# Expert weights in eleven slots at the start, selection of tokens in halves, and a TensorE product in each ranking round

## The chip, the cores and the metric

The kernel runs on one core of a Trainium2 chip. The metric is the device time of one execution in microseconds (us). Three executions of the kernel before took 2456.19, 2457.54 and 2457.84 us, with a median of 2457.54.

## The reference, cut to what matters

Two transformer blocks run one after the other on 512 tokens of width 1024. The change touches only the end of the second block: the router, the experts and the last layer norm.

```python
def expert_choice_ffn(x, w_router, w_gate_up, w_down):
    cap = EC_CAPACITY_FACTOR * T // N_EXPERTS            # 2 * 512 // 16 = 64
    logits = einsum('btd,de->bte', x, w_router)
    aff = softmax(logits, axis=-1)                       # 512 tokens x 16 experts
    gate, idx = lax.top_k(swapaxes(aff, 1, 2), cap)      # each expert takes its 64 best tokens
    xs = x[bidx, idx]
    h = einsum('becd,edf->becf', xs, w_gate_up)          # 1024 -> 2048, per expert
    hg, hu = split(h, 2, axis=-1)
    ye = einsum('becf,efd->becd', silu(hg) * hu, w_down) # 1024 -> 1024
    return zeros_like(x).at[bidx, idx].add(ye * gate)

x = layer_norm(DN_ALPHA * x + mix, ln1_g, ln1_b)
ffn = expert_choice_ffn(x, w_router, w_gate_up, w_down)
x = layer_norm(DN_ALPHA * x + ffn, ln2_g, ln2_b)
```

## The kernel before, in words

Everything is float32 on one core. After the first block and the attention of the second, the stage that matters here begins at about 1907 us of the span. It runs in this order.

**Layer norm and router.** The product with w_out_2 ends in the signal `m31`, the normalised rows stand in `XR` (signal `x31` for the last of them), and the logits are ready with `logits`. VectorE makes the affinities `affN` (L3029 to L3034), and TensorE transposes them into a bank, 16 experts by 512 tokens (L2169, signal `affT`).

**Selection.** VectorE ranks in eight rounds over 16 partitions of 512 elements: `max` gives the eight best (L3038), `match_replace` overwrites them with -1 (L3039). What has become negative is chosen; a running sum (`tensor_tensor_scan`, L3042) numbers the chosen tokens, TensorE turns the numbers back to token order (L2173, signal `posN`), and `choose(0)` builds the selection matrix `SP` (L3056) and the gate matrix `SG` (L3058). While VectorE ranks, TensorE has nothing to do.

**Experts.** Experts are taken in pairs, p = 0 to 7. In each pair TensorE does four groups `q` of gate-and-up products (`rows`, L2251), gathers the next pair's tokens (`gather`, L2198), turns the activations (L2284), does two halves of the down product (`down`, L2289), and scatters the results (L2235, L2236); VectorE adds them to `acc` (L3104). In pair 0 the gather (`first_gather`, L2184) is exact and interleaved with the groups.

**Weights.** A pair needs 12 pieces of 2 MB, so there are 96 pieces, c = 0 to 95. They come through a ring of nine slots (`eslot`, `ES = 9`). SyncE issues all loads in one order, and each waits for the group that used its slot nine pieces ago (L690), so piece 20 waits for `group5.0` and pieces 21 and 22 for `group0.1`. Pieces 0 to 2 are issued after `br23.1` (1907 us), then the two rows of the first layer norm's gain and bias (`ln1_g_2`, `ln1_b_2`, L683, into the upper half of `acc`), pieces 3 to 6 after `m31`, piece 7 after `logits`, piece 8 after `posN`; its slot shares its memory with the ranking's tiles. Pieces 9 and 10 come in halves after `half0.0` and `group0.0`.

**Residual and end.** Right after `choose(0)` VectorE writes the scaled residual, ALPHA times the normalised row with gain and bias, into `acc` (`residual`, L3131 and L3133). In the last pair TensorE reads `acc` into the eight output banks with identity products (`kept`, L2220): two of them stand ahead of the last group `q = 3` of gate-and-up, the others around the down products. The last norm then works from those banks.

Of the kernel before, what the change touches and what calls it, by code (L numbers as in the profile page):

```python
# [5 lines left out]
F32, F32R = mybir.dt.float32, mybir.dt.float32r  # L6
# [6 lines left out]
NT = SEQ // P  # L13
# [85 lines left out]
def build(nc, T, out):  # L99
    with ExitStack() as ctx:  # L100
# [3 lines left out]
        def sig(name, step=1):  # L104
            return Sig(nc, ctx, name, step)
# [20 lines left out]
        def carve(t, start, shapes):  # L126
# [97 lines left out]
        (slot4, SGT, SP, xst, ga, actT, ye, acc, posN, affN, m8, lmax, lsum, slot8), at_e = carve(work, 0, [  # L224
            (KB, 512), (512,), (NT, P), (KB, P), (2, 512), (KB, P), (2, 512), (NT, DM),
            (NT, NE), (NT, NE), (8,), (NT,), (NT,), (KB, 512)])
        (affT, wrk, cum), _ = carve(work, at_e - 4096, [(512,), (512,), (512,)])
        assert at_e <= 17560
        lnrow = acc[:, 2:4, :]
        (slot5, slot6, iota, wr, wr2, wb, ln_col), at_e = carve(work, 17560, [(KB, 512), (KB, 512), (EC,), (KB, NE), (KB, HB), (NE,), (2, KB)])  # L230
        fold, wr_b = cols[:, 0:NE], cols[:, 32:160].rearrange("p (k e) -> p k e", k=KB)
        assert at_e <= 26500
        (SG,), at_e = carve(const, 2 * P, [(NT, P)])
        assert at_e <= 6 * P
        SPT, ye_hi, ye_lo, lgT = SGT, ye, ga, cum
# [3 lines left out]
        eslot = [slot5, slot6, ring[2], ring[0], ring[1], ring[3], slot4, AT, slot8]  # L239
        ES = len(eslot)  # L240
        lnrow2 = eslot[(12 * NE // 2 - 8) % ES].rearrange("p k n -> p (k n)")[:, 0:2 * DM].rearrange("p (a b) -> p a b", a=2)

        LAST = 12 * NE // 2 - 2

        def weights(c, at):

            return eslot[c % ES].rearrange("p k n -> p (k n)")[:, at:at + 512]
# [37 lines left out]
        e_w, e_h = [sig(f"expert_weights{q}", 16) for q in range(ES)], [sig(f"expert_halves{q}", 16) for q in range(2)]  # L285
# [174 lines left out]
        def _(sp):  # L460
# [203 lines left out]

            def load_half(sem, c, h, what):
                to, part = eslot[c % ES].rearrange("p k n -> p (k n)"), slice(h * 2048, h * 2048 + 2048)
                sem.mark(sp.dma_start(to[:, part], expert_rows(c // 12, c % 12)[:, part]), what)
            for c in range(12 * NE // 2):
                if c in (ES, ES + 1):
                    if c == ES:  # L670
                        for h in range(2):
                            sp.wait_ge(*e_pe(("half0.0", "group0.0")[h]))
                            for e in range(2):
                                load_half(e_w[(c + e) % ES], c + e, h, f"h{c + e}" if h == 0 else f"w{c + e}")
                    continue
                if c >= ES:
                    sp.wait_ge(*e_pe(f"group{(c - ES) % 12 // 2}.{(c - ES) // 12}"))
                elif c < 3:
                    sp.wait_ge(*mg_pe("br23.1"))
                elif c < 7:  # L680
                    if c == 3:
                        for n, name in enumerate(("ln1_g_2", "ln1_b_2")):
                            l_row.mark(sp.dma_start(lnrow[:, n, :], T[name].broadcast_to([P, DM])), name)  # L683
                    sp.wait_ge(*l_pe("m31"))
                elif c == 7:
                    sp.wait_ge(*q_pe("logits"))
                else:
                    sp.wait_ge(*q_pe("posN"))
                if c < LAST:
                    e_w[c % ES].mark(sp.dma_start(eslot[c % ES].rearrange("p k n -> p (k n)"), expert_rows(c // 12, c % 12)), f"w{c}")  # L690
                elif c == LAST:
                    sp.wait_ge(*e_pe(f"group{(c + 1 - ES) % 12 // 2}.{(c + 1 - ES) // 12}"))
                    for h in range(2):
                        for e in range(2):
                            load_half((e_h if h == 0 else e_w)[e if h == 0 else (c + e) % ES], c + e, h, f"{'hw'[h]}{c + e}")
# [132 lines left out]
        def _(act):  # L828
# [684 lines left out]
            for q in range(4):  # L1513
                first_T(q)
                high(act, e_act, XH[:, q, :], XR[:, q, :], f"XH{q}")
# [20 lines left out]
        def _(pe):  # L1536
# [631 lines left out]
            for t in range(NT):  # L2168
                mm = pe.transpose(psum[3][0:NE, t * P:(t + 1) * P], affN[:, t, :], ident)  # L2169
            q_pe.mark(mm, "affT")  # L2170
            pe.wait_ge(*q_vec("pos"))
            for t in range(NT):
                mm = pe.transpose(psum[2][:, t * NE:(t + 1) * NE], cum[0:NE, t * P:(t + 1) * P], ident[0:NE, 0:NE])  # L2173
            q_pe.mark(mm, "posN")
# [65 lines left out]
            def experts(p):  # L2240
                last = p == NE // 2 - 1

                def loaded(q):
                    for e in range(2):
                        c = 12 * p + 2 * q + e
                        pe.wait_ge(*e_w[c % ES](f"w{c}"))
# [7 lines left out]
                for q in range(4):  # L2254
# [20 lines left out]
                    if p == 0 and q == 0:  # L2275
                        e_pe.mark(mm, "half0.0")
# [27 lines left out]
                for k in range(4):  # L2304
                    for n in range(2):
                        mm = down(0, k, n)
                e_pe.mark(mm, f"group4.{p}")
# [31 lines left out]
        def _(dve):  # L2339
# [685 lines left out]
            q_vec.link(dve, dve.memset(affT[0:NE, :], 1.0))  # L3025
# [20 lines left out]
            q_vec.link(dve, dve.tensor_copy(posN, psum[2][:, 0:NT * NE].rearrange("p (t e) -> p t e", t=NT)))  # L3046
# [13 lines left out]
            def experts(p):  # L3060
# [7 lines left out]
                if not last:  # L3068
                    choose(p + 1)
                if p == 0:  # L3070
# [20 lines left out]
                for m in range(2 * NT):  # L3091
# [4 lines left out]
                    elif last:  # L3096
                        final_stats(t)
                        if t:
                            final_inv(t - 1)
                    else:  # L3100
                        a = acc[:, t, n * 512:(n + 1) * 512]
                        if p:
                            dve.wait_ge(*e_vec(f"acc{m}.{p - 1}"))
                        e_vec.mark(dve.tensor_tensor(a, psum[scatter_banks[m]][:, :], a, ALU.add), f"acc{m}.{p}")  # L3104
# [24 lines left out]
            def residual(t, tmp):  # L3129
                n = XR[:, t, :].rearrange("p (j q) -> p q j", j=KB)  # L3130
                q_vec.link(dve, dve.scalar_tensor_tensor(tmp.rearrange("p (q j) -> p q j", j=KB), n, ALPHA, lnrow[:, 0, :].rearrange("p (q j) -> p q j", j=KB),  # L3131
                                                         ALU.mult, ALU.mult))
                q_vec.mark(dve.scalar_tensor_tensor(acc[:, t, :], lnrow[:, 1, :], ALPHA, tmp, ALU.mult, ALU.add), f"acc{t}")  # L3133
            choose(0)
            dve.wait_ge(*l_row("ln1_b_2"))
            y_row = ye.rearrange("p a n -> p (a n)")
            residual(0, acc[:, 0, :])
            residual(1, acc[:, 1, :])
            dve.wait_ge(*l_act("x31"))
            q_vec.link(dve, dve.scalar_tensor_tensor(y_row.rearrange("p (q j) -> p q j", j=KB), XR[:, 3, :].rearrange("p (j q) -> p q j", j=KB), ALPHA,  # L3140
                                                     lnrow[:, 0, :].rearrange("p (q j) -> p q j", j=KB), ALU.mult, ALU.mult))
            residual(2, acc[:, 2, :])
            q_vec.mark(dve.scalar_tensor_tensor(acc[:, 3, :], lnrow[:, 1, :], ALPHA, y_row, ALU.mult, ALU.add), "acc3")
            for t in range(NT):
                dve.wait_ge(*q_vec(f"acc{t}"))
# [104 lines left out]
```

## Time and profile before

| | before |
|---|---|
| median of three executions | 2457.54 us |
| the profiled execution's own time | 2456.17 us |
| its span | 2454.4 us |
| TensorE busy (matmul) | 2373.1 us, 97% |
| VectorE busy | 1137.8 us, 46% |
| ScalarE busy | 869.1 us, 35% |
| DMA, mean over the span | 163 GB/s |
| expert weights | 96 pieces of 2 MB |

A matmul's end is modelled in the trace, so a busy TensorE is not TensorE at its peak. The share of busy time is a mean over stages with different limits, and the stage of the change is the last fifth of the span. PEclk is the granted TensorE clock as a share of 2.4 GHz: 1.00 is 2.4 GHz and 0.50 is 1.2 GHz.

### The profile page before, as it was taken

How to read it: one execution, taken by the hardware profiler on the slowest of the kernel's cores; microseconds unless marked ns; L12 is line 12 of the kernel's file. 1: busy time of each engine (PE TensorE's matmuls, PEld its weight loads, DVE VectorE, ACT ScalarE, POOL GpSimd, SP SyncE). 2: the span in 40 equal slices, each digit the busy share in tenths (PEclk: the TensorE clock that was granted, in tenths of full speed). 3: DMA queues.
4: the chain of work that ended last, by engine and by line, in shares of the span. 5: the costliest groups of instructions: out<-in, count | busy, mean ns of one | idle time of the engine just before them, and what ended most of it. 6: DMA issues, size and time to landing. Idle time of an engine off the chain costs nothing.

```text
span 2454.4 us, 31324 instructions
## 1 busy us (share of the span) xinstructions
PE 2373.1 (97%) x13306; PEld 1760.8 (72%) x13306; DVE 1137.8 (46%) x1595; ACT 869.1 (35%) x1403; POOL 124.3 (5%) x130
## 2 busy tenths in 40 slices
PE   8999999999999999999999999998999979999997
PEld 6788878888887888888888888865788733443332
DVE  6857676354543324354344463668433552131113
ACT  7554544243433323243233343347322411111111
POOL 0303021100000000000000001200000000000000
PEclk9999999999999999999999999999999989999998
DMA  5121313232224333242222332321322589999996
GB/s 168 70 73 67 104 54 111 70 121 87 102 86 155 120 108 136 79 158 79 93 103 103 112 138 103 115 105 48 127 96 78 200 346 416 429 427 430 428 429 260
DMA packets 117386, 400.97 MB, mean 163 GB/s; under 512 B 6656, under 2 KB 24704, under 8 KB 104320
## 3 DMA queue, kind: packets, MB, share of 16 engines
q1 hardware_dynamic: 113088, 384.29, 40.7%
q0 software_dynamic: 4160, 14.68, 1.7%
q8 instruction: 106, 1.74, 0.3%
q14 instruction: 32, 0.26, 0.0%
HBM read 385.06 MB, written 13.89 MB: 163 GB/s over the span
## 4 chain that ended last, share of the span: by engine, by line
PE 83%; DVE 7%; DMA 6%; ACT 3%; issue 1%; SPq 0%; POOL 0%; DVEq 0%; ACTq 0%; POOLq 0%
PE banks L94 20%; PE banks L96 19%; PE banks L95 19%; PE banks L2251 7%; PE banks L2289 5%; DMA activations_T<-w_gate_up_in 1%; DMA ring<-w_gate_up_in 1%; DMA work<-w_gate_up_in 1%; DVE ring_split L88 1%; DMA work<-o_b 1%; PE banks L1653 1%; DMA ring<-w_up_in 1%; PE banks L1665 1%; PE banks L2030 1%; PE banks L1683 1%
## 5 line engine op out<-in xcount | busy, mean ns | idle before, releaser
L94 PE MATMUL banks<-work_split,ring_split 128*128 128x512 f32 (+1 forms) x1560 | 617.4, 396 | 2.4 <-issue 0.8
L88 DVE TENSOR_TENSOR ring_split<-ring,halves_split 128x1024 fp32r<-128x1024 f32 x281 | 353.5, 1268 | 523.3 <-ACT halves_split L83 522.9
L95 PE MATMUL banks<-work_split,halves_split 128*128 128x512 f32 x1512 | 588.8, 389 | 0.0
L96 PE MATMUL banks<-activations_T_split,halves_split 128*128 128x512 f32 x1160 | 452.3, 390 | 0.0
L83 ACT ACTIVATE halves_split<-ring 128x1024 fp32r<-128x1024 f32 x281 | 293.7, 1055 | 310.9 <-PE banks L96 236.5
L94 PEld LDWEIGHTS banks<-work_split,ring_split 128*128 128x128 f32 x1560 | 293.0, 188 | 70.1 <-issue 8.1
L95 PEld LDWEIGHTS banks<-work_split,halves_split 128*128 128x128 f32 x1512 | 284.1, 188 | 55.7 <-issue 0.5
L96 PE MATMUL banks<-ring_split,work_split 128*128 128x512 f32 (+1 forms) x704 | 270.8, 385 | 0.0
L95 PE MATMUL banks<-halves_split,work_split 128*128 128x512 f32 x672 | 261.6, 389 | 0.0
L96 PEld LDWEIGHTS banks<-activations_T_split,halves_split 128*128 128x128 f32 x1160 | 217.7, 188 | 46.2
L2251 PE MATMUL banks<-work 128*64 128x512 f32 x464 | 150.7, 607 | 4.9 <-DMA work<-w_gate_up_in 2.6
L94 PE MATMUL banks<-halves_split,work_split 128*128 128x512 f32 x384 | 150.1, 391 | 1.9 <-DVE ring_split L88 1.9
L96 PEld LDWEIGHTS banks<-ring_split,work_split 128*128 128x128 f32 x704 | 132.2, 188 | 26.4
L95 PEld LDWEIGHTS banks<-halves_split,work_split 128*128 128x128 f32 x672 | 126.2, 188 | 25.7
L96 PE MATMUL banks<-work_split,halves_split 128*128 128x512 f32 x352 | 137.0, 389 | 0.0
L88 DVE TENSOR_TENSOR work_split<-work,work_split 128x1024 fp32r<-128x1024 f32 (+2 forms) x98 | 101.6, 1066 | 36.7 <-ACT work_split L83 36.7
L94 PE MATMUL banks<-halves_split,activations_T_split 128*128 128x512 f32 x288 | 114.7, 398 | 0.0
L3078 DVE TENSOR_TENSOR work<-banks,work 128x512 f32<-128x512 f32 x16 | 10.3, 687 | 198.1 <-ACT work L1498 198.1
L2251 PE MATMUL banks<-ring,work 128*64 128x512 f32 x336 | 94.6, 609 | 5.1 <-DMA ring<-w_gate_up_in 2.8
L2251 PEld LDWEIGHTS banks<-work 128*64 128x64 f32 x464 | 47.2, 140 | 72.7 <-issue 72.7
L83 ACT ACTIVATE work_split<-work 128x1024 fp32r<-128x1024 f32 (+2 forms) x98 | 87.9, 926 | 29.3 <-PE banks L1702 10.5
L1498 ACT ACTIVATE work<-banks 128x512 f32<-128x512 f32 x16 | 8.7, 597 | 251.9 <-PE banks L2251 251.9
(387 smaller groups left out, 3166.6 us busy)
## 6 DMA issues: line engine op xcount, KB each, us to landing
ring<-w_in_in SPq DMA_DIRECT2D x30, 2048.0 KB, 7.7
work<-w_gate_up_in SPq DMA_DIRECT2D x29, 2048.0 KB, 26.8
ring<-w_gate_up_in SPq DMA_DIRECT2D x21, 2048.0 KB, 26.2
ring<-w_down_in SPq DMA_DIRECT2D x19, 2048.0 KB, 9.2
work<-w_down_in SPq DMA_DIRECT2D x11, 2048.0 KB, 27.0
ring<-w_in_in SPq DMA_DIRECT2D x17, 1024.0 KB, 7.7
ring<-w_up_in SPq DMA_DIRECT2D x8, 2048.0 KB, 7.9
activations_T<-w_gate_up_in SPq DMA_DIRECT2D x8, 2048.0 KB, 26.9
```

The lines of the kernel that those rows point to most:

```text
L83: s.mark(act.activation(R(dst), src, ACT.Copy), what)
L88: s.mark(dve.tensor_tensor(R(dst), src, R(hi).bitcast(F32), ALU.subtract), what)
L94: pe.matmul(out, R(ll), R(rh), start=start, stop=False)
L95: pe.matmul(out, R(lh), R(rh), start=False, stop=False)
L96: return pe.matmul(out, R(lh), R(rl), start=False, stop=stop)
L1653: mm = pe.matmul(bank_a[j][x, c], NMd[j][h, t, :], Yd[j][h, t, :], start=True, stop=True)
L1665: x_mm = pe.matmul(bank_b[j][x, c], PP[j][x, t, :], X[j][x, t, :], start=True, stop=True)
L1683: mm = pe.matmul(V, Y[j][:, t, :], vb[:, j, t, :], start=True, stop=(t == 0))
L2030: mm = pe.transpose(turned_at(fam, i)[:, s, k * P:(k + 1) * P], probs_at(fam, i)[:, s, k * P:(k + 1) * P], ident)
L2251: mm = pe.matmul(psum[3 + c % 2 * 2 + c // 2][64 * e:64 * e + 64, :], xst[:, 2 * q + k, 64 * e:64 * e + 64], weights(12 * p + 2 * q + e, k ...
L2289: mm = pe.matmul(psum[4 + n][64 * e:64 * e + 64, :], actT[:, 4 * a + k, 64 * e:64 * e + 64], weights(12 * p + 8 + 2 * a + e, k * DM + n * ...
L3078: e_vec.mark(dve.tensor_tensor(g, psum[4 + 2 * f][:, :].rearrange("p (q k) -> p k q", k=4), g, ALU.mult), f"ga{f}.{p}")
```

## The change

1. **Slots.** Two more regions serve as weight slots, each once: `XH` (the high parts of the rows, not needed before pair 0's gathers) holds piece 0, `acc` holds piece 10. After that the ring has nine slots as before, in the order given by `slot_no` and `former`. Four pieces are issued after `br23.1`, pieces 4 to 7 and 10 after `m31`, piece 8 after `logits`, piece 9 after `x31`. During pair 0 the next loads are issued in halves.
2. **Residual.** Since `acc` holds weights in pair 0, the residual is no longer written first. Pair 0's results are copied into `acc` (no add). The gain and bias rows are loaded into `XH` late, between the issues of pieces 90 and 91, behind a wait for `whole3`: four additions on VectorE in pair 6 that restore the full rows in `XR`. The residual is then added in `keep()`, on VectorE in the last pair, and `kept(n, t)` waits for it.
3. **Selection.** The 512 tokens of each expert lie as two halves of 256 in partitions 0 to 15 and 32 to 47. Eight rounds rank each half (the last without `match_replace`), and the two sorted lists are joined into the 64th best value, the threshold. TensorE spreads the threshold, VectorE marks the tokens above and equal to it, and four products with a triangle and with ones number them, with a fifth for ties.
4. **A product per round.** TensorE multiplies the identity with 512 columns of `XR` into a bank that nobody reads, once after each of the eight rounds.

```diff
+        lnrow, kept_tmp = XH[:, 0:2, :], XH[:, 2:4, :]
+        def slot_no(c):
+            return ES if c == 0 else ES + 1 if c == ES + 1 else (c - 1 if c <= ES else c - ES - 2) % ES
+        def former(c):
+            return c - ES - 1 if c <= 2 * ES + 1 else c - ES
...
+            for c in range(4):
+                load(c)
+            sp.wait_ge(*l_pe("m31"))
+            for c in range(4, 8):
+                load(c)
+            load(ES + 1)
+            sp.wait_ge(*q_pe("logits"))
+            load(8)
+            sp.wait_ge(*l_act("x31"))
+            load(ES)
...
+                if (n, p) == (5, NE // 2 - 2) and freed(c - 1) != (n, p):
+                    sp.wait_ge(*e_vec("whole3"))
+                    for n, name in enumerate(("ln1_g_2", "ln1_b_2")):
+                        l_row.mark(sp.dma_start(lnrow[:, n, :], T[name].broadcast_to([P, DM])), name)
...
+            for r in range(EC // 8):
+                pe.wait_ge(*q_vec(f"round{r}"))
+                pe.matmul(psum[0][:, :], ident, XR[:, 0, 0:512], start=True, stop=True)
+            pe.wait_ge(*q_vec("thr"))
+            q_pe.mark(pe.transpose(psum[2][:, 0:NE], thr_row[0:NE, 0, :], ident[0:NE, 0:NE]), "thr")
+            pe.wait_ge(*q_vec("marks"))
+            pe.matmul(psum[1][:, 0:2 * NT * NE], m_incl, marks.rearrange("p a t e -> p (a t e)"), start=True, stop=False)
...
             def kept(n, t):
-                pe.wait_ge(*e_vec(f"acc{4 * n + t}.{NE // 2 - 2}"))
+                pe.wait_ge(*e_vec(f"kept{t}"))
...
             for r in range(EC // 8):
-                left = wrk[0:NE, :] if r else psum[3][0:NE, :]
-                q_vec.link(dve, dve.max(m8[0:NE, :], left))
-                q_vec.link(dve, dve.match_replace(wrk[0:NE, :], m8[0:NE, :], left, -1.0))
-            q_vec.link(dve, dve.tensor_scalar(wrk[0:NE, :], wrk[0:NE, :], 0.0, None, ALU.is_lt))
-            q_vec.link(dve, dve.tensor_tensor_scan(cum[0:NE, :], affT[0:NE, :], wrk[0:NE, :], 0.0, ALU.mult, ALU.add))
-            q_vec.mark(dve.tensor_tensor(cum[0:NE, :], cum[0:NE, :], wrk[0:NE, :], ALU.mult), "pos")
+                left = wrk[0:48, :] if r else psum[3][0:48, 0:256]
+                m8 = best[0:48, 8 * r:8 * r + 8]
+                q_vec.mark(dve.max(m8, left), f"round{r}")
+                dve.wait_ge(*q_vec(f"round{r}"))
+                if r < EC // 8 - 1:
+                    q_vec.link(dve, dve.match_replace(wrk[0:48, :], m8, left, -1.0))
...
+                if p == NE // 2 - 2:
+                    for t in range(NT):
+                        e_vec.mark(dve.tensor_tensor(XR[:, t, :], R(XR[:, t, :]).bitcast(F32), R(XH[:, t, :]).bitcast(F32), ALU.add), f"whole{t}")
...
+            def keep():
+                dve.wait_ge(*l_row("ln1_b_2"))
+                for t in range(NT):
+                    tmp = kept_tmp[:, t % 2, :]
+                    turned = lambda x: x.rearrange("p (q j) -> p q j", j=KB)
+                    e_vec.link(dve, dve.scalar_tensor_tensor(turned(tmp), XR[:, t, :].rearrange("p (j q) -> p q j", j=KB), ALPHA, turned(lnrow[:, 0, :]), ALU.mult, ALU.mult))
+                    for m in (t, NT + t):
+                        dve.wait_ge(*e_vec(f"acc{m}.{NE // 2 - 2}"))
+                    e_vec.link(dve, dve.tensor_tensor(acc[:, t, :], acc[:, t, :], tmp, ALU.add))
+                    e_vec.mark(dve.scalar_tensor_tensor(acc[:, t, :], lnrow[:, 1, :], ALPHA, acc[:, t, :], ALU.mult, ALU.add), f"kept{t}")
```

`keep()` is called in the last pair right after VectorE has built that pair's scatter matrix, ahead of the products `ga0.7` and `ga1.7` (L3078).

## Rows read from the trace of the kernel before

**Rows 1.** The page, section 2: bytes moved in 40 slices of 61 us

```profile
GB/s 168 70 73 67 104 54 111 70 121 87 102 86 155 120 108 136 79 158 79 93 103 103 112 138 103 115 105 48 127 96 78 200 346 416 429 427 430 428 429 260
```

**Rows 2.** Busy time by stretch: length, engines' busy us (x instructions), PEclk, DMA share, GB/s

```profile
2100.00:2200.00 100.00, 99.35 (x468) 39.38 (x464) 17.58 (x29) 12.25 (x27) 0.00 (x0) 1.00 1.01 428
2300.00:2400.00 100.00, 93.35 (x417) 37.69 (x417) 20.12 (x32) 11.85 (x26) 0.00 (x0) 0.97 1.01 428
```

**Rows 3.** Waits of TensorE from 1980 us on: total us, times, longest

```profile
PE banks L2251 <- DMA ring<-w_gate_up_in: 2.8, 1, 2.8
```

**Rows 4.** Timeline of SyncE, and a stretch of two microseconds

```profile
2053.72 0.93 SPq L690 DMA_DIRECT2D ring<-w_down_in  x2
...
2054.00:2056.00 2.00, 2.00 (x12) 0.66 (x10) 0.00 (x0) 0.00 (x0) 0.00 (x0) 1.00 0.80 229
```

**Rows 5.** Timeline of VectorE, selection and residual: start us, us, what, [idle before]

```profile
1964.97 0.69 DVE L3038 MAX8 work<-banks 16x8 f32<-16x512 f32 x1 [1.11 <-PE banks L2169]
1965.69 0.08 DVE L3039 MATCH_VALUE_LOAD work<-work,banks 16x8 f32 x1
1965.77 0.67 DVE L3039 MATCH_REPLACE8 work<-work,banks 16x512 f32<-16x512 f32 x1
1966.47 0.68 DVE L3038 MAX8 work<-work 16x8 f32<-16x512 f32 x1
...
1980.25 0.69 DVE L3056 TENSOR_TENSOR work_split<-work 128x512 fp32r<-128x512 f32 x1
...
1981.59 1.93 DVE L3131 SCALAR_TENSOR_TENSOR work<-residual,work 128x1024 f32<-128x1024 f32 x1
1983.55 1.23 DVE L3133 SCALAR_TENSOR_TENSOR work<-work 128x1024 f32<-128x1024 f32 x1
```

**Rows 6.** VectorE's groups by form: busy us, mean ns

```profile
L2495 DVE COPY work<-banks 128x256 f32<-128x256 f32 x8 | 3.4, 422 | 3.1 <-PE banks L1701 3.1
...
L3000 DVE TENSOR_TENSOR const<-work 128x128 f32<-128x128 f32 x1 | 0.3, 290 | 0.0
...
L3046 DVE COPY work<-banks 128x64 f32<-128x64 f32 x1 | 0.2, 225 | 0.7 <-PE banks L2173 0.7
```

**Rows 7.** Timeline of TensorE from the affinities to the first group

```profile
1963.91 1.02 PE L2169 MATMUL banks<-const,work 128*16 128x128 f32 x4 [1.67 <-DVE work L3034]
1979.34 0.61 PE L2173 MATMUL banks<-const,work 16*128 16x16 f32 x4 [14.41 <-DVE work L3043]
1980.99 5.49 PE L2184 MATMUL banks<-work_split,residual 128*128 128x128 f32 x24 [1.04 <-DVE work_split L3056]
```

**Rows 8.** Two stretches of one microsecond, columns as in rows 2

```profile
1963.00:1964.00 1.00, 0.09 (x1) 0.09 (x2) 0.62 (x3) 0.13 (x1) 0.00 (x0) 0.51 0.81 344
1986.00:1987.00 1.00, 1.00 (x5) 0.48 (x5) 0.96 (x2) 0.57 (x1) 0.00 (x0) 0.54 0.43 180
```

**Rows 9.** The chain that ended last, pair 0: start us, us

```profile
1993.73 1.98 PE banks L2184 x16
```

**Rows 10.** The chain that ended last, end of pair 7

```profile
2396.65 8.70 PE banks L2251 x32
2405.35 1.91 PE banks L2220 x4
2407.26 7.04 PE banks L2251 x32
```

**Rows 11.** DMA issues at 2367.2 us (piece 90) and at L683: us to landing

```profile
work<-w_gate_up_in SPq DMA_DIRECT2D x1, 2048.0 KB, 34.2
...
DMA to landing us min/median/max: 18.2/19.1/20.0
```

**Rows 12.** DMA issues at 1910.06 us (piece 2), us to landing; L683's second issue

```profile
ring<-w_gate_up_in SPq DMA_DIRECT2D x1, 2048.0 KB, 17.6
...
L683 SPq DMA_DIRECT2D work<-ln_b_in x1: 484/484/484, 1911.1 to 1911.1; - x1
```

**Rows 13.** Timeline of VectorE in pair 6, its wait ahead of the scatter

```profile
2373.84 0.75 DVE L3088 SCALAR_TENSOR_TENSOR work_split<-banks,const,work_split 128x512 fp32r<-128x512 f32 x1 [13.11 <-ACT work_split L1512]
```

More of the change, by code:

```diff
@@ L663, in expert_rows, with flat @@
                 return WGU[e][q] if q < 4 else WDN[e][q - 4]
+            def flat(c):
+                return eslot[slot_no(c)].rearrange("p k n -> p (k n)")
             def load_half(sem, c, h, what):
[L666 to L686, printed above, removed]
-                else:
[L688 to L692, printed above, removed]
@@ new lines, in load_half, with load, freed @@
+                part = slice(h * 2048, h * 2048 + 2048)
+                sem.mark(sp.dma_start(flat(c)[:, part], expert_rows(c // 12, c % 12)[:, part]), what)
+            def load(c):
+                e_w[slot_no(c)].mark(sp.dma_start(flat(c), expert_rows(c // 12, c % 12)), f"w{c}")
+            def freed(c):
+                return former(c) % 12 // 2, former(c) // 12
+            for c in range(4):
[3 more added lines that the diff above has]
+                load(c)
@@ new lines, in _ @@
+            load(ES + 1)
[3 more added lines that the diff above has]
+            load(ES)
+            c = ES + 2
+            while former(c) < 10:
+                cs = [n for n in (c, c + 1) if freed(n) == freed(c)]
+                for h in range(2):
+                    sp.wait_ge(*e_pe(("half", "group")[h] + f"{freed(c)[0]}.0"))
+                    for n in cs:
+                        load_half(e_w[slot_no(n)], n, h, f"h{n}" if h == 0 else f"w{n}")
+                c += len(cs)
@@ new lines, in _ @@
+            for c in range(c, LAST + 1):
+                n, p = freed(c if c < LAST else c + 1)
+                if (n, p) == (5, NE // 2 - 2) and freed(c - 1) != (n, p):
+                    sp.wait_ge(*e_vec("whole3"))
+                    for n, name in enumerate(("ln1_g_2", "ln1_b_2")):
+                        l_row.mark(sp.dma_start(lnrow[:, n, :], T[name].broadcast_to([P, DM])), name)
+                    n, p = freed(c)
+                sp.wait_ge(*e_pe(f"group{n}.{p}"))
+                if c < LAST:
+                    load(c)
+                else:
@@ L1512, in experts @@
                     e_act.mark(act.activation(R(ye_hi[:, n, :]), psum[4 + n][:, :], ACT.Copy, scale=gcol[:, p % 2:p % 2 + 1]), f"y{n}.{p}")
-            for q in range(4):
+            first_T(0)
+            for q in range(1, 4):
                 first_T(q)
+                if q == 1:
+                    act.wait_ge(*e_pe("group0.0"))
+                    high(act, e_act, XH[:, 0, :], XR[:, 0, :], "XH0")
                 high(act, e_act, XH[:, q, :], XR[:, q, :], f"XH{q}")
@@ L2167, in _ @@
             pe.wait_ge(*q_vec("aff"))
-            for t in range(NT):
-                mm = pe.transpose(psum[3][0:NE, t * P:(t + 1) * P], affN[:, t, :], ident)
+            for u in range(2):
+                mm = pe.transpose(psum[3][0:HB, u * P:(u + 1) * P], wide[:, u * HB:(u + 1) * HB], ident)
             q_pe.mark(mm, "affT")
[L2171 to L2174, printed above, removed]
+            for r in range(EC // 8):
[5 more added lines that the diff above has]
+            pe.matmul(psum[1][:, 0:2 * NT * NE], m_incl, marks.rearrange("p a t e -> p (a t e)"), start=True, stop=False)
+            at = psum[1][:, 0:2 * NT * NE].rearrange("p (a t e) -> p a t e", a=2, t=NT)
+            for t in range(NT - 1):
+                pe.matmul(at[:, :, t + 1:, :], ones, marks[:, :, t:t + 1, :].broadcast_to([P, 2, NT - 1 - t, NE]), start=False, stop=False)
+            pe.wait_ge(*q_vec("above"))
+            q_pe.mark(pe.matmul(at[:, 1, :, :], thr_row[0:NE, 1, :], ident[0:NE, 0:NE].unsqueeze(1).broadcast_to([NE, NT, NE]), start=False, stop=True), "posN")
             def first_gather(blocks):
@@ L2245, in loaded @@
                         c = 12 * p + 2 * q + e
-                        pe.wait_ge(*e_w[c % ES](f"w{c}"))
+                        pe.wait_ge(*e_w[slot_no(c)](f"w{c}"))
                 def rows(q, k):
@@ L2274, in experts @@
                     mm = rows(q, 0)
-                    if p == 0 and q == 0:
-                        e_pe.mark(mm, "half0.0")
+                    if p == 0:
+                        e_pe.mark(mm, f"half{q}.0")
                     e_pe.mark(rows(q, 1), f"group{q}.{p}")
@@ L2306, in experts @@
                         mm = down(0, k, n)
+                    if p == 0 and k == 1:
+                        e_pe.mark(mm, "half4.0")
                 e_pe.mark(mm, f"group4.{p}")
@@ L3069, in experts @@
                     choose(p + 1)
+                else:
+                    keep()
                 if p == 0:
```

67 lines of the change are left out of this document (36 added, 31 removed).

## The prediction

> **What bounds the kernel now.** I read the page first. Its bytes by slice [rows 1] show where the stage of the change lies and what limits it: from the thirty-fourth slice to the second last the core moves 416 to 430 GB/s, and nowhere else does it come near that. The busy times by stretch say the same of the expert stage: 428 GB/s with a DMA share of 1.01, while TensorE is at 99% of one stretch and 93% of the other [rows 2]. So two things lie close together. A pair of experts needs 12 pieces of 2.097 MB, 25.2 MB, which at 428 GB/s is 58.8 us, 4.90 us a piece. TensorE is ahead of that need at first, at 99% busy; it uses up the nine filled slots, and later waits for pieces [rows 3].
>
> Then I looked for the point at which the stream of pieces is tied to TensorE. It is at 2053.7 us. There SyncE issues pieces 21 and 22, which waited for `group0.1`, and in the two microseconds after it the rate is only 229 GB/s [rows 4]: the DMA engines had finished piece 20 and had nothing left. From there on they never run dry. 69 pieces, 21 to 89, take 338 us at 4.90, which gives 2392 us, plus a few for the first descriptor and the completion; the group that needs piece 89 starts at 2396.65 [rows 10]. So the late part of the kernel is fixed by **when `group0.1` ends, plus 343 us**.
>
> After 2396.65 TensorE goes on nearly without a gap: q = 2 in 8.70 us, two `kept` products 1.91, q = 3 in 7.04 [rows 10]. The 8.70 against 7.04 is a clock that had dropped in the wait. Each later piece lands a little ahead of its use: piece 90 is issued at 2367.2 and lands 34.2 later, at 2401.4 [rows 11]; piece 91, one piece on, lands at about 2406.3, 1.0 ahead of 2407.26. So whatever is put in front of q = 3 and is longer than this chain costs its full length.
>
> **The two extra slots: worth nothing in the sum.** They let the DMA engines move pieces 9 and 10 before pair 0, 9.8 us of stream. But neither is used again. Piece 20 again needs `group5.0` and pieces 21 and 22 again need `group0.1`, the same events as before, by `former`. The stream is thus further ahead in pair 0, stands still longer before `group0.1` (by my count some 7 us instead of under 1 [rows 4]), and starts again at the same event. Only an earlier `group0.1` counts. The other end, that the slots pay, is a rival below. The halves in pair 0 fall to the same argument.
>
> **Selection.** All times here are the old trace's. The affinities need two transposes instead of four that took 1.02 [rows 7], so ranking starts at 1964.45 instead of 1964.97. A round was 1.50 from one `max` to the next [rows 5]. The price of halving comes from VectorE's other forms: 128 elements 290 ns, 256 elements 422 ns [rows 6], which is 1.03 ns an element; it makes 0.26 less for each of the two operations, 0.97 a round. That 48 partitions work instead of 16 adds nothing, if I go by those rows of 128 partitions. Eight rounds without the last `match_replace` (0.5) are 7.3, ending at 1971.7. Three operations on 64 elements (0.25 each with their gap [rows 6]) and a copy of 128 (0.3) give the threshold at 1972.8. Over TensorE and back I take 0.35 (four small transposes took 0.61 [rows 7]), two marks 0.5, then the three operations that count the ones above, 0.8, which cover the four numbering products; the fifth product 0.4, and two operations 0.55. `SP` would start at 1975.4 instead of 1980.25 [rows 5]: **4.85 earlier, if TensorE is on time**.
>
> **The product in each round.** It is an identity product with 512 columns like a `kept`, of which two take 1.91 [rows 10]: 0.955 each at 2.4 GHz, about 1.85 at 1.2. A round is 0.97, so at the full clock they just keep up. But the clock has already dropped when they begin: at 1963 to 1964 it is granted at 0.51, after TensorE ran out of work, and when dense work begins again at 1980.99 it stays low until late in 1986 [rows 7, 8], 5.9 us. In the later case q = 2 lost 1.66, that is 3.3 us at half speed [rows 10]. The first product starts at 1964.9. If the clock returns 5.0 us on, 2.7 products are done by then, and the other 5.3 take 5.1: TensorE is free at 1975.0, **2.2 late** for the threshold's transpose. With 3.3 us it is 1.3 late, with 5.9 it is 2.6. The gain of `SP` shrinks to 2.65.
>
> What the products buy is the clock for the gather. 24 instructions of it took 5.49 at half speed [rows 7]; 16 take 1.98 at full speed [rows 9], so 24 would be 2.97, 2.5 less. Between the last product and the gather lie some 3 us in which TensorE has only short work, and it was after such a stretch that the clock fell at 1963 [rows 8]. So the gain lies between 0 and 2.5; with nothing to choose by I take 1.25. The first group then starts **3.9 earlier** (the ends: 2.2, with the clock lost again and 2.6 late, to 7.4, with no lateness and a full-speed gather). Pair 0 has its weights in time, as piece 9 lands at about 1987, and the residual's operations that leave VectorE there were hidden behind a wait that ended only with the scatter matrix. So `group0.1`, and with it the arrival of piece 89, comes 3.9 earlier.
>
> **The residual at the end.** Before, the gain and bias rows moved at 1910 to 1931 us, when the DMA engines had time, and the residual's 13 us on VectorE stood in pair 0 where VectorE had nothing else. Now both stand in the last pair. The rows are issued right behind piece 90, at 2367.7 in old time, with some 34 us of stream ahead of them. At L683 the bias row was issued at 1911.1 and landed 20.0 later, at 1931.1 [rows 11, 12], and piece 2 ahead of it, issued at 1910.06, landed at 1927.7 [rows 12], so 3.4 apart; by bytes alone 1 MB is 2.45. I take 3.0: the rows are there at 2404.4. `whole3` is early enough: VectorE stands idle for 13.11 us ahead of 2373.84 in pair 6 [rows 13], and four additions of 1.25 fit in.
>
> `keep()` costs 1.96 for the turned product, 1.25 for the addition and 1.25 for the second scaling [rows 5] (the addition priced as the second scaling), 4.4 a block. `kept0` comes at 2408.9, `kept1` at 2413.3, `kept3` at 2422.0. TensorE ends q = 2 at 2405.35, waits 3.5 for the first, works 1 us, and waits about 3.4 for the second. q = 3 can start at 2414.25 instead of 2407.26: **7.0 later**. After two waits of 3.4 the clock will be down as it was at 2396 after one of 2.66, so 0.85 more for the `kept` and 1.66 for q = 3: **9.5 later** in all. VectorE is done with `keep()` at 2422.0, before q = 3 ends at 2423.8, so `ga0.7` adds nothing. Piece 91 lands 2.45 later, 2408.7, hidden behind the wait; if that cover were gone it would cost 1.4. What follows moves along unchanged.
>
> The Trainium skill (DMA: Bandwidth & Descriptors, section Queues, rings and completion order) says that descriptors start in ring order on each DMA engine, but that completion is not first in, first out for an issuing engine. By it the rows could be complete with piece 90, at 2401.4, and the wait would cost 6.5 instead of 9.5. The trace's one case has the bias row 3.4 behind its piece [rows 11, 12].
>
> **Sum.** 2456.17 (the profiled execution's time) - 3.9 + 9.5 = 2461.8; I say 2462. The profiled execution lies 1.4 below the median of the runs shown, so against that median it is 0.2% more or a little less. 0.2% is 4.9 us, about what a measurement of this kernel can tell from no change.
>
> **Rivals.**
> 1. *The slots pay.* If the stream did not stand still before `group0.1`, it would be ahead for the rest. TensorE could win back at most its waits for pieces, some 12 us over the last three pairs (one group of them in [rows 3]). 2456.2 - 12 - 3.9 + 9.5 = 2449.8. For it: the rate of 428 right after [rows 2]. Against it: `former(21)` is 12, and the dip at 2054 [rows 4]. It decides if the rate in pair 0 stays at 428 up to `group0.1`. 12%.
> 2. *The residual is covered.* The rows land early, say by 2396.5, and `kept1` is ready by 2405.4. Then only piece 91's 1.4 is left: 2453.7, and 2450.2 with the large end of the selection. Against it: a queue of 34 us ahead of them [rows 11]. 15%.
> 3. *The products stay at the low clock.* Eight at 1.85 from 1964.9 end at 1979.7, 6.9 late; the selection then loses 2.1, the gather gains 2.5 or nothing: 2465.3 to 2467.8. For it: they come one by one, and the clock needed 5.9 us of dense work [rows 8]. Against it: at half speed a product is longer than a round, so there is no gap between them. 7%.
>
> **Chances.** The forecast has 66%; its own range is 2457 (selection's large end, tail 7.0) to 2465 (small end, 10.4). Of it 37 are slower by over 0.2%, 28 within, 1 faster. Rival 1 gives 9 faster and 3 within, rival 2 gives 4 and 11, rival 3 gives 7 slower. Together: faster 0.14, within 0.42, slower 0.44. The range for 8 in 10 is 2451 to 2468.
>
> **What would show it.** Right: PEclk near 0.5 under the first products and 1.0 under the last; the threshold's transpose waiting 1 to 3 us for TensorE; `SP` 2 to 3 us earlier in the span; a DMA rate near zero for some 7 us before `group0.1`; then 428 to the end; `kept` at the last pair waiting for VectorE twice, 3.4 us each, and q = 3 of pair 7 some 9.5 us further from q = 2 than now. Wrong: no wait ahead of `kept`, a rate that never falls in pair 0, or pair 1 starting more than 7 us earlier.

## The result, and the profile after

| | before | changed |
|---|---|---|
| median of 20 executions | 2456.61 us | 2461.25 us |
| the profiled execution's own time | 2456.17 us | 2459.51 us |
| its span | 2454.4 us | 2457.7 us |

The ratio of the changed kernel to the one before is 1.0018, with a 95% interval of 1.0013 to 1.0024. That is 4.4 us slower. It is a small step, but the whole interval lies above 1. One execution of the changed kernel was disturbed (2647.74 us) and is left out of the ratio and of the spread told below. The two profiled spans are 3.3 us apart: the changed kernel's profiled execution is 1.7 under its median, that of before 0.4.

In the page's first two sections the stage of the change looks almost as before [rows 1]. One slice dips to 367 GB/s:

```profile
PE 2381.6 (97%) x13327; PEld 1764.2 (72%) x13327; DVE 1142.0 (46%) x1608; ACT 867.2 (35%) x1403; POOL 124.2 (5%) x130
...
GB/s 168 70 76 63 103 59 106 70 120 95 98 82 160 114 118 134 81 148 90 82 103 103 112 146 95 120 102 45 137 86 86 224 408 367 429 428 429 428 428 212
```

The selection in VectorE's timeline, to be laid beside [rows 5]:

```profile
1964.89 0.42 DVE L3081 MAX8 work<-banks 48x8 f32<-48x256 f32 x1 [0.50 <-PE banks L2201]
1965.35 0.08 DVE L3084 MATCH_VALUE_LOAD work<-work,banks 48x8 f32 x1
1965.43 0.41 DVE L3084 MATCH_REPLACE8 work<-work,banks 48x256 f32<-48x256 f32 x1
1965.87 0.42 DVE L3081 MAX8 work<-work 48x8 f32<-48x256 f32 x1
...
1972.83 0.21 DVE L3089 COPY work<-work 16x128 f32<-16x128 f32 x1
1974.40 0.22 DVE L3092 TENSOR_TENSOR work<-work,banks 128x64 f32<-128x64 f32 x1 [1.35 <-PE banks L2207]
...
1976.86 0.69 DVE L3110 TENSOR_TENSOR work_split<-work,const 128x512 fp32r<-128x512 f32 x1
```

A round is 0.98 us, and the threshold's row is ready at 1973.04. TensorE's timeline of the same stretch, beside [rows 7]:

```profile
1964.44 0.41 PE L2201 MATMUL banks<-const,work 128*64 128x128 f32 x2 [1.67 <-DVE work L3076]
1965.37 8.83 PE L2205 MATMUL banks<-residual,const 128*128 128x512 f32 x16 [0.52 <-DVE work L3081]
1974.13 0.23 PE L2207 MATMUL banks<-const,work 16*128 16x16 f32 x1
...
1977.61 2.94 PE L2224 MATMUL banks<-work_split,residual 128*128 128x128 f32 x24 [1.36 <-DVE work_split L3110]
```

The first group (q = 0 of pair 0), before and changed:

```profile
1986.41 7.32 PE L2251 MATMUL banks<-work 128*64 128x512 f32 x32
...
1980.65 0.61 PE L2291 MATMUL banks<-rows_high,work 128*64 128x512 f32 x1
```

The eight products keep TensorE until 1974.13, so the threshold waits 1.1 us for it. The gather runs at full speed, 2.94 instead of 5.49 [rows 7], and the first group starts at 1980.65 instead of 1986.41. From the first transpose of the affinities (1964.44 and 1963.91 [rows 7]) to the first group it is 16.2 us instead of 22.5.

What the DMA engines do in the stretch before `group0.1` (length, busy us by engine, PEclk, DMA share, GB/s):

```profile
2042.00:2044.00 2.00, 2.00 (x12) 0.63 (x10) 1.97 (x4) 0.00 (x0) 0.00 (x0) 1.00 0.07 25
2044.00:2048.00 4.00, 4.00 (x22) 1.37 (x20) 0.17 (x1) 0.00 (x0) 0.00 (x0) 1.00 0.00 0
2048.00:2050.00 2.00, 2.00 (x12) 0.64 (x10) 0.00 (x0) 0.00 (x0) 0.00 (x0) 1.00 0.69 172
```

They move nothing for some six microseconds, until SyncE issues piece 21, beside [rows 4]:

```profile
2047.70 0.33 SPq L687 DMA_DIRECT2D work<-w_down_in  x1
```

The longest waits of TensorE behind the selection have a new first row (total us, times, longest), which [rows 3] did not have:

```profile
PE banks L2260 <- DVE work L3200: 7.2, 2, 4.9
PE banks L2291 <- issue: 6.1, 3, 2.6
PE banks L2291 <- DMA halves<-w_gate_up_in: 2.8, 1, 2.8
```

And the chain that ended last, in the last pair, where it was TensorE alone before [rows 10]:

```profile
2363.37 34.27 DMA rows_high<-ln_b_in
...
2397.66 1.92 DVE rows_high L3196
...
2399.60 1.24 DVE work L3199
...
2403.95 1.24 DVE work L3199
...
2405.21 1.24 DVE work L3200
...
2406.49 2.07 PE banks L2260 x2
2408.57 9.07 PE banks L2291 x32
```

Read in order of time, the chain begins with the bias row's transfer, goes through VectorE's `keep()`, and reaches TensorE at the second `kept`, L2260. The group q = 3 behind it takes 9.07 us instead of 7.04: the granted clock is 0.50 from 2404 to 2412 us, after TensorE had stood idle for 4.86 and 2.35 us. The group q = 2 ahead of the waits starts at 2390.28, from TensorE's timeline:

```profile
2390.28 0.61 PE L2291 MATMUL banks<-halves,work 128*64 128x512 f32 x1 [1.12 <-issue]
```

Its weights, piece 89, were issued at 2362.05 and landed 28.1 us later, at 2390.15.

### The profile page after: what moved, and what is told of

The parts are those of the page before. It is cut to its first block, busy times and chain, and to the rows that moved or that the text cites. A ratio compares the mean times of both kernels' runs of the same rounds, so it can differ in the third digit from the quotient of the medians.

```text
span 2457.7 us, 31386 instructions
## 1 busy us (share of the span) xinstructions
PE 2381.6 (97%) x13327; PEld 1764.2 (72%) x13327; DVE 1142.0 (46%) x1608; ACT 867.2 (35%) x1403; POOL 124.2 (5%) x130
## 4 chain that ended last, share of the span: by engine, by line
PE 82%; DMA 7%; DVE 6%; ACT 3%; issue 1%; SPq 0%; DVEq 0%; ACTq 0%
PE banks L94 20%; PE banks L96 20%; PE banks L95 20%; PE banks L2291 6%; PE banks L2329 4%; DMA rows_high<-ln_b_in 1%; DMA work<-w_down_in 1%; DMA halves<-w_gate_up_in 1%; DMA work<-w_gate_up_in 1%; DMA work<-o_b 1%; DVE ring_split L88 1%; PE banks L1685 1%; DMA ring<-w_up_in 1%; DVE const L2911 1%; PE banks L1697 1%
## 5 line engine op out<-in xcount | busy, mean ns | idle before, releaser
L2291 PE MATMUL banks<-work 128*64 128x512 f32 x416 | 158.4, 608 | 3.6 <-issue 2.4
L2291 PE MATMUL banks<-ring,work 128*64 128x512 f32 x352 | 113.9, 598 | 5.5 <-DMA halves<-w_gate_up_in 2.8
L2291 PEld LDWEIGHTS banks<-work 128*64 128x64 f32 x416 | 49.3, 140 | 57.7 <-issue 57.7
```

The lines of the kernel that those rows point to most:

```text
L2291: mm = pe.matmul(psum[3 + c % 2 * 2 + c // 2][64 * e:64 * e + 64, :], xst[:, 2 * q + k, 64 * e:64 * e + 64], weights(12 * p + 2 * q + e, k ...
```

## The experiments

Each ratio is to runs of the kernel before on the same chip. There were three such groups, e1 to e4, then e5, e6, e8 and e9, then e10 and e12, each on a chip of its own, so kernels of different groups are compared by their ratios and not by their medians. e2 has five executions, the other experiments nine to eleven. A single profile has one trap here. The stage ahead of the router, which none of the kernels changes, ended between 1963.5 and 1968.2 us in the twelve profiles. So places in profiles are counted from the first transpose of the affinities, and the spans of single profiles are not compared. "First group" is the start of q = 0 in pair 0 from that transpose, "end" is the span's end from it, both in us. One profile's end also carries the clock that the last groups happened to get, some 1.5 us.

| kernel | ratio to before, 95% interval | first group | end |
|---|---|---|---|
| before | | 22.5 | 490.5 |
| changed | 1.0018 (1.0013 to 1.0024) | 16.2 | 493.3 |
| e1 rows first | 1.0002 (0.9994 to 1.0011) | 16.2 | 485.7 |
| e6 rows first again | 0.9989 (0.9980 to 0.9997) | 16.8 | 486.5 |
| e2 old selection | 1.0038 (1.0025 to 1.0052) | 21.6 | 497.4 |
| e3 selection only | 0.9985 (0.9977 to 0.9994) | 17.3 | 485.2 |
| e4 no products | 1.0024 (1.0015 to 1.0032) | 18.2 | 493.6 |
| e5 late 9 and 10 | 1.0015 (1.0006 to 1.0024) | 17.5 | 493.3 |
| e8 early products | 0.9975 (0.9965 to 0.9984) | 17.6 | 485.4 |
| e9 selection, no products | 0.9978 (0.9969 to 0.9988) | 18.0 | 486.8 |
| e10 products throughout | 0.9978 (0.9969 to 0.9987) | 15.2 | 484.0 |
| e12 both | 0.9985 (0.9976 to 0.9994) | 15.2 | 485.5 |

**The rows ahead of piece 89.**

```diff
-                if (n, p) == (5, NE // 2 - 2) and freed(c - 1) != (n, p):
+                if (n, p) == (4, NE // 2 - 2) and freed(c - 1) != (n, p):
```

> The gain and bias rows are issued ahead of pieces 89 and 90 instead of behind them; all the rest is the changed kernel. Theory (the rows' place in the queue is what costs): the rows are complete 2.5 us behind piece 88, so keep() runs under q = 2 of the last pair; piece 89 comes 2.45 later. TensorE no longer waits for kept, and q = 3 starts when piece 91 is there. 8 us less than the changed kernel: about 2453, under before. Rival (VectorE's 17 us of keep() in the last pair are the cost wherever the rows stand): no more than 2 us less than the changed kernel.

VectorE's timeline of this kernel's last pair, and the waits of TensorE from 2380 us to the end:

```profile
2391.41 1.96 DVE L3196 SCALAR_TENSOR_TENSOR rows_high<-residual,rows_high 128x1024 f32<-128x1024 f32 x1 [10.22 <-DMA rows_high<-ln_b_in]
...
2399.02 1.22 DVE L3200 SCALAR_TENSOR_TENSOR work<-rows_high,work 128x1024 f32<-128x1024 f32 x1
```

```profile
PE banks L2291 <- issue: 3.5, 1, 3.5
PE banks L2324 <- DVE work L3134: 0.4, 1, 0.4
```

The wait for `kept` is gone: `kept1` is done at 2400.2, and q = 2 ends at 2404.86. Counted from the affinities the end comes 7.6 us earlier than in the changed kernel (8 were expected). Its median, 2455.66, was 2.7 over what I had expected, and the same as that of before on this chip. In this profile the stage ahead took 3.7 us more than in the changed kernel's. Among the waits of VectorE between 1600 and 1720 us is one of 4.8 us, for a load of the attention's bias:

```profile
DVE work L2922 <- DMA work<-na_bias_in: 4.8, 1, 4.8
```

The same wait is 2.2 us in the profile of before and 2.1 in the changed kernel's, so 2.7 of the 3.7 us are there. To see whether this belongs to the kernel, I ran it again, unchanged:

> The kernel with the gain and bias rows ahead of piece 89, once more. Its first profile had a stage ahead of the router that took 3.7 us more than in the other profiles, behind a wait for a load of the attention's bias. Theory (that wait comes and goes from run to run): counted from the affinities' transpose the end is again 4.8 us earlier than before and 7.6 earlier than in the changed kernel, whatever the stage ahead took. Rival (this kernel has the wait each time): the stage ahead is 3 us or more longer again.

The ratio was 0.9989, the wait for the bias load was 2.2 us, the stage ahead was 2.5 us shorter than in the first profile, and the end came 4.0 earlier than before and 6.8 earlier than in the changed kernel (4.8 and 7.6 were expected; the first group was 0.6 later). So that wait comes and goes, and the rival fell, though the stage was still 1.2 us longer than in the changed kernel. By the ratios (1.0002 and 0.9989 against 1.0018) the two runs lie 4 and 7 us under the changed kernel.

With the rows there in time, VectorE's 17 us of work in the last pair cost nothing: from the start of q = 2 of pair 7 to the end it is 57.5 us in e1 and 57.7 in e6, against 57.8 before and 67.4 in the changed kernel. What remains is the rows' own 1 MB, now ahead of piece 89. From the issue of piece 21 to the start of that q = 2 it is 344.9 us in e6 and 345.0 in e1, against 342.6 in the changed kernel.

**The old selection in the changed kernel.** The selection's blocks of before (ranking over 512, running sum, four transposes) stand in place of the new ones, and the products are gone; the ranking's tiles lie where the changed kernel has its own.

> The changed kernel's slots and residual with the old selection, no products in the rounds. Theory (selection gives some 6 us, the slots nothing, the residual costs 9.7): 6 to 6.5 us over the changed kernel, 2467, and some 10 over before. Rival (the slots pay what the residual costs): 2457 to 2461.

1.0038: by the ratios slots and residual alone cost 9.3 us, with an interval of 6 to 13, and the selection gives 5 back. Both are a little under what I had expected (10 and 6 to 6.5). In the profile they are smaller still: the end is 6.9 us later than before and 4.1 later than in the changed kernel, with q = 3 of pair 7 at 7.69 us and not 9.07.

**The selection alone.** The slots, the order of the loads and the residual are those of before. Only the selection is new:

```diff
+            for r in range(EC // 8):
+                pe.wait_ge(*q_vec(f"round{r}"))
+                pe.matmul(psum[0][:, :], ident, XR[:, 0, 0:512], start=True, stop=True)
...
             def kept(n, t):
                 pe.wait_ge(*e_vec(f"acc{4 * n + t}.{NE // 2 - 2}"))
```

> The kernel before with only the new selection and its products; nine slots and the residual in pair 0 as before. Theory: the first group of pair 0 and everything behind it 6 to 6.5 us earlier, 2450, with nothing given back at the end. Rival (part of the 6 us came from the extra slots): 2452 to 2454.

0.9985, 2451.65: by the ratios 3.7 us under before, with an interval of 1.5 to 5.6, and 8 us under the changed kernel. The median lies between theory and rival. The gather took 4.23 us in this profile, not 2.94, so its first group is 1.1 later than in the changed kernel; that, and not the missing slots, is what the profile is short of the 6 us. The end came 5.3 earlier than before, and the first group 5.2: in the profile all of it arrives at the end.

**No products.** The changed kernel without them.

```diff
-            for r in range(EC // 8):
-                pe.wait_ge(*q_vec(f"round{r}"))
-                pe.matmul(psum[0][:, :], ident, XR[:, 0, 0:512], start=True, stop=True)
```

> The changed kernel without the eight products in the ranking rounds. Theory: the threshold's transpose is no longer late (1.1 us gained), but the small products (0.4) and the gather (2.5) run at 1.2 GHz: 1.8 us over the changed kernel, 2463, and the first group 1.8 later behind the affinities. Rival (the products cost as much as they give): within 0.5 us of the changed kernel.

The first group is 2.0 later, as the theory has it, with a gather of 4.59 us. Of the time nothing is shown: 1.0024 and 1.0018 lie within each other's intervals. In the profile the end is only 0.3 later, because the last pair's q = 3 took 7.64 us instead of 9.07.

**The extra slots filled late.**

```diff
-            load(ES + 1)
             sp.wait_ge(*q_pe("logits"))
             load(8)
-            sp.wait_ge(*l_act("x31"))
+            sp.wait_ge(*e_pe("half0.0"))
             load(ES)
+            load(ES + 1)
```

> The changed kernel, but pieces 9 and 10 are issued only after half0.0, so that the two extra slots are filled no earlier than before. Theory (the extra slots give nothing): counted from the first transpose of the affinities the end is within 1 us of the changed kernel's, and the DMA engines' pause before group0.1 is about 10 us shorter in return. Rival (the slots give part of the gain): 3 us or more longer.

The end is the same to 0.1 us, and the ratio nearly (1.0015). That the ends agree so closely is partly luck: the first group was 1.3 us later here, since the eight products took 9.89 us, and q = 3 of pair 7 took 7.94 us instead of 9.07. The steadier measure is the stretch between. From the first group to the start of q = 2 of pair 7 it is 409.5 us here and 409.6 in the changed kernel. The pause has shrunk, to about 3 us:

```profile
2044.00:2048.00 4.00, 4.00 (x20) 1.29 (x18) 2.79 (x5) 0.00 (x0) 0.00 (x0) 1.00 0.92 389
2048.00:2050.00 2.00, 2.00 (x12) 0.72 (x10) 0.00 (x0) 0.00 (x0) 0.00 (x0) 1.00 0.10 41
2050.00:2052.00 2.00, 2.00 (x12) 0.71 (x10) 0.00 (x0) 0.00 (x0) 0.00 (x0) 1.00 0.57 123
```

That is about 3 us less, not 10. Another 2 us of stream were made up earlier in pair 0: from 2020 to 2040 us the engines move 422 GB/s here and 379 in the changed kernel. The rest is not accounted for.

**Selection alone, with other products.** First without any:

> The kernel before with the new selection only and without products. Theory: 1.5 to 1.9 us over selection only with its products of 512 columns (first group 18.1 us behind the affinities' transpose), and about 3 over the one with early products; 4.4 us under before. Rival: no difference between the three.

The first group came at 18.0, where 18.1 was expected. In the time there is no difference: 0.9978, with the products 0.9985 (e3), and 0.9975 for the kernel that follows (e8), intervals that overlap. So the rival holds for the times.

Then with two before the affinities and narrower ones in the rounds:

```diff
+            for n in (512, 256):
+                pe.matmul(psum[0][:, 0:n], ident, XR[:, 0, 0:n], start=True, stop=True)
             pe.wait_ge(*q_vec("aff"))
...
-                pe.matmul(psum[0][:, :], ident, XR[:, 0, 0:512], start=True, stop=True)
+                pe.matmul(psum[0][:, 0:384], ident, XR[:, 0, 0:384], start=True, stop=True)
```

> The kernel before with the new selection only; two products (512 and 256 columns) already between the logits and the affinities, and 384 columns instead of 512 in each round. Theory: the clock does not fall before the rounds, the threshold's transpose is not late, the gather runs at 2.4 GHz: 1.1 us less than selection only with the gather at full speed, up to 2.4 less where its gather ran partly at 1.2 GHz: the first group 15.1 us behind the affinities' transpose, 2449 to 2450. Rival (the clock falls anyway in the selection's small steps): the same as selection only.

I had missed where the clock falls. With early products it holds through the rounds and then drops in the small steps behind them, just ahead of the gather:

```profile
1966.00:1968.00 2.00, 1.70 (x4) 0.59 (x4) 1.86 (x7) 0.00 (x0) 0.00 (x0) 1.00 1.05 451
...
1976.00:1977.00 1.00, 0.09 (x1) 0.00 (x0) 0.81 (x3) 0.00 (x0) 0.00 (x0) 0.74 0.88 377
1978.00:1980.00 2.00, 2.00 (x12) 2.00 (x11) 1.97 (x2) 0.00 (x0) 0.00 (x0) 0.50 1.01 418
```

The gather took 5.49 us again, as in the kernel before, and the first group came at 17.6, not 15.1. The rival was right on this. The ratio, 0.9975, was all the same the lowest of all kernels, which shows how little the times tell of steps of 2 us here. So products were added there too:

```diff
             q_pe.mark(pe.transpose(psum[2][:, 0:NE], thr_row[0:NE, 0, :], ident[0:NE, 0:NE]), "thr")
+            pe.matmul(psum[0][:, 0:128], ident, XR[:, 0, 0:128], start=True, stop=True)
             pe.wait_ge(*q_vec("marks"))
...
             q_pe.mark(pe.matmul(at[:, 1, :, :], thr_row[0:NE, 1, :], ident[0:NE, 0:NE].unsqueeze(1).broadcast_to([NE, NT, NE]), start=False, stop=True), "posN")
+            pe.matmul(psum[0][:, :], ident, XR[:, 0, 0:512], start=True, stop=True)
```

> Selection only, on the slots and the residual of before, with products in each place where TensorE waits: 512 and 256 columns before the affinities, 384 a round, 128 behind the threshold's transpose, 512 behind the numbering. Theory (what the early products did not keep was the clock in the small steps behind the rounds): the granted clock stays at 1.0 from the logits to the gather, the gather takes 2.94, the first group starts 15.1 to 15.5 us behind the affinities' transpose, 7 earlier than before, and the time is about 2 us under the one with early products: ratio to before about 0.997. Rival (the time is set elsewhere): no less than selection only without products.

```profile
1976.36 2.94 PE L2202 MATMUL banks<-work_split,residual 128*128 128x128 f32 x24 [0.31 <-DVE work_split L3086]
1979.40 2.79 PE L2269 MATMUL banks<-work 128*64 128x512 f32 x12
```

The gather is at full speed and the first group at 15.2, 7.3 earlier than before. The end came 6.5 earlier. By measured time it is 2450.71, ratio 0.9978, and no less than without products (0.9978), as the rival has it: the intervals overlap, and whether the products are worth their 1 to 3 us in the median stays open.

**Both together.** The changed kernel with the rows first and with these products:

> The changed kernel with the rows ahead of piece 89 and with the same products throughout. Theory: the same first group, 15.1 to 15.5 us behind the affinities' transpose; against the one with the slots and the residual of before only the rows' 1 MB in the stream remains, 2.5 us more, ratio about 0.998. Rival (the slots pay once nothing is given back): not slower than the other.

0.9985 against 0.9978, and the end 1.5 us later from the same first group. The sign is as expected in both; the size in the profile is 1.5, not 2.5, and the intervals of the ratios overlap. The slots and the late residual, with the wait taken out of them, give no gain.

## Why the prediction was right

The forecast was 2462 (2461.8 in the sum), 5.6 us over the profiled time of before; measured were 4.4 us by the ratio and 3.3 in the profiled spans. The mechanism held: the tie, the idle slots, the late threshold and the two waits for `kept` are all in the profile. The number is closer than its terms deserve. Counted from the affinities, the profile has 6.3 us gained up to the first group (3.9 said), 0.6 up to q = 2 of pair 7 (nothing said) and 9.7 lost behind it (9.5 said), so 2.8 in all and not 5.6. The forecast's own range has a slip, too: the selection's large end with a tail of 7.0 gives 2455.8 from the profiled time, not 2457, and where the 10.4 of the other end comes from the prediction does not say.

**The tie at `group0.1`.** Right. Piece 21 is issued 6.0 us earlier in the span, and from there to the group that needs piece 89 it is 342.6 us (2047.70 to 2390.28), as in the kernel before (2053.72 to 2396.65, 342.9). The other profiles say the same. In all twelve, with nine slots or eleven, piece 21 is issued 67.0 to 67.4 us behind the first group, and q = 2 of pair 7 starts 342.4 to 343.9 us later where the rows are not ahead of piece 89, 344.9 to 345.3 where they are (e1, e6, e12).

**The slots.** Right that they are worth next to nothing, shown by the stretches above, by e5 and by the pause of six microseconds in the profile (some 7 were foreseen). From the first group to q = 2 of pair 7 the changed kernel needs 0.6 us less than before (409.6 and 410.2), some of it ahead of the issue of piece 21 (67.0 and 67.3) and some behind. Why is not shown; the selection alone (e3) needs 410.1.

**The selection.** The rounds and the small steps were as worked out (a round 0.98 for 0.97, threshold ready 8.6 us behind the first transpose for 8.9). The products were late by 1.1 us instead of 2.2. I had the clock down when they begin; in this profile it was still granted at 1.00 up to 1965.25, fell as the first product began (1965.37), and was back about 3.5 us behind that and not 5. And the gather ran wholly at 2.4 GHz, a gain of 2.5 us where I took the middle of 0 and 2.5. `SP` starts 3.4 us earlier in the span, where 2 to 3 were foreseen. **The term that was mis-sized is "the first group then starts 3.9 earlier"**: it was 6.3 in this profile, inside the ends given (2.2 to 7.4). In the other profiles with eight products of 512 columns it was 5.0 to 6.3, as the clock fell or didn't.

**The residual at the end.** Right in place, kind and nearly in size. The bias row landed at 2397.67, 2.6 behind piece 90 (3.0 foreseen, 2.45 by bytes). TensorE waited 4.9 and 2.4 us for `kept0` and `kept1` (3.5 and 3.4 foreseen). From the start of q = 2 to the end of q = 3 it is 27.3 us instead of 17.65, so **9.7 later; 9.5 was said**. That the sizes agree so well is luck, for the pieces differ: q = 2 ran at full speed this time, after a wait of 1.1 us and not 2.7, and won 1.6; the two `kept` products took 1.91 and 2.07 us and lost 2.1 together, not 0.85; q = 3 lost 2.0 and not 1.66. From the start of q = 2 to the end of the span three other profiles with the rows behind piece 90 lose 8.3 (e2, e4) and 8.6 (e5) against before. e1 and e6 show the cause by taking it away.

**On the page of the Trainium skill** (DMA: Bandwidth & Descriptors, section Queues, rings and completion order): it says that completion is not first in, first out for an issuing engine. The trace agrees, but only for one of the two rows. From issue to landing, for piece 90 (issued at 2362.42) and the gain row (at 2362.90):

```profile
activations_T<-w_gate_up_in SPq DMA_DIRECT2D x1, 2048.0 KB, 32.7
...
rows_high<-ln_g_in SPq DMA_DIRECT2D x1, 512.0 KB, 31.7
```

So piece 90 landed at 2395.1 and the gain row, issued after it, at 2394.6; in e2, e4 and e5 the gain row is 0.3 to 0.4 us ahead in the same way. The bias row, for which `keep()` waits, took 34.3 us and came 2.5 to 2.6 us behind piece 90 in all four profiles. The case that would have brought the wait down to 6.5 did not occur.

**The rivals.** The slots pay: fallen, by e5 and by e12, which has the slots and is not under e10, which has not. The residual is covered: fallen for the changed kernel, and it is what e1 makes true by order alone. The products stay at the low clock: fallen, for the clock returned within the rounds (PEclk, two stretches of the changed kernel):

```profile
1966.00:1968.00 2.00, 2.00 (x3) 0.64 (x2) 1.86 (x7) 0.00 (x0) 0.00 (x0) 0.50 0.97 418
1968.00:1969.00 1.00, 1.00 (x3) 0.47 (x2) 0.93 (x4) 0.00 (x0) 0.00 (x0) 0.55 1.08 459
```

The difference between 3.3 us in the spans and 4.4 in the ratio I take for the spread of single runs: the changed kernel's times lie between 2458.4 and 2464.7, and in the other profiles with eight products of 512 columns the first group gained 5.0 to 6.3 us, never more than in this one. That is argued, not shown.

## What to carry to other kernels

Buffers that are used once only move the stream's idle time; ask which event restarts the stream after them, and whether it comes earlier. When work leaves an early stage to make room, follow it to where it lands: here 1 MB of rows behind a queue of 34 us put VectorE's work on two blocks, 4.4 us each, in front of the last group of gate-and-up, and an earlier place in the issue order undid it. A part that gains is worth running alone: the selection without the rest has the ratio 0.9985 to before, the combination 1.0018.

## What the runs showed that I had not expected

The stage ahead of the router, alike in all kernels, ended anywhere from 1963.5 to 1968.2 us in twelve profiles, more than the effect that was being measured. The late ones were not all explained. One wait for a bias load was 4.8 us in the latest (e1) and 3.6 in the second latest (e12), and 2.0 to 2.8 in the other ten.

What keeps the clock up to the gather is not settled. With products before and in the rounds (e8), TensorE stood idle for 1.36 us ahead of the gather, the granted clock fell to 0.50 and the gather took 5.49 us. With the same 1.36 us of idle time ahead of it the changed kernel kept 1.00 and its gather took 2.94:

```profile
1976.00:1978.00 2.00, 0.64 (x5) 0.50 (x5) 1.61 (x4) 0.00 (x0) 0.00 (x0) 1.00 1.07 459
```

With products in the small steps as well the idle time was 0.31 us, and the gather took 2.94 in both profiles (e10, e12). The same eight products in the rounds took from 8.80 to 9.89 us in five profiles, and the gather behind them 2.94 in four and 4.23 in one (e3). Two profiles are not enough to say that filling every wait always keeps the clock.

The 512 KB gain row landed 0.3 to 0.5 us ahead of the 2 MB piece issued before it, in all four profiles that have it behind piece 90. In the profile of before, where it follows piece 2, it landed 1.1 us behind that piece.
